# Weight rings begun one stage ahead, and a compression over 128 partitions, in a three-layer transformer kernel

## The reference

```python
mq, mk, mv, nq, nkv, ng = split(h @ w_in)            # layer 0: sparse mixer, 2840 columns
o = concat(moba_attention(...), nsa_attention(...)); o @ w_out
q, k, v = split(h @ w_in)                            # layer 1: difference attention, 3072 columns
# layer 2: gated delta rule over 512 positions; then 16,384 experts, 16 per head and token, by product keys
(silu(h @ w_gate) * (h @ w_up)) @ w_down             # feed-forward of layers 0 and 1, 2816 hidden

def nsa_compress(t, pos_emb, w1, w2):                # t: [b, g, S, 64]
    idx = arange(ncmp)[:, None] * 16 + arange(32)    # 15 blocks of 32 positions
    blocks = t[:, :, idx] + pos_emb
    hid = silu(einsum('bgnld,lde->bgne', blocks, w1))      # sum over 32 positions x 64 channels, e = 256
    return einsum('bgne,ed->bgnd', hid, w2)
```

## Time and profile before

| what | before |
|---|---|
| median of 3 runs | 2494.89 us |
| the profiled execution: its time, its span | 2503.65 us, 2501.9 us |
| PE (matmul) busy | 2059.2 us, 82% |
| PEld (weight load) busy | 1847.1 us, 74% |
| DVE busy | 1667.4 us, 67% |
| ACT busy | 934.1 us, 37% |
| POOL busy | 101.0 us, 4% |
| HBM read, mean rate | 363.87 MB, 150 GB/s |
| span of `cmp` | 183.3 to 276.3 us |

### The profile page before, as it was taken

How to read it: one execution, slowest core, us unless ns; L and a number is a source line. 1 busy time by engine, 2 the same in 40 slices (tenths; PEclk the granted TensorE clock), 3 DMA queues, 4 the chain that set the end, 5 groups by cost and what they waited for, 6 DMA issues and landing times. The chain is left out here.

```text
span 2501.9 us, 41554 instructions
## 1 busy us (share of the span) xinstructions
PE 2059.2 (82%) x16664; PEld 1847.1 (74%) x16664; DVE 1667.4 (67%) x2773; ACT 934.1 (37%) x1334; POOL 101.0 (4%) x92
## 2 busy tenths in 40 slices
PE   5838578996745999697887876899876999999997
PEld 2838358995735899486877765899865777999996
DVE  2562767876876786676356564389997777666665
ACT  1310434433342433333244452445465333444443
POOL 1000000000000000241000110000000000000000
PEclk9865699998967999898699887999999999999999
DMA  5707149875303884232000013377501666555554
GB/s 185 286 14 171 59 138 343 307 257 184 120 4 119 322 321 173 94 109 85 3 2 4 3 48 140 122 230 221 170 0 65 211 217 214 205 191 186 185 185 143
DMA packets 167334, 377.46 MB, mean 151 GB/s; under 512 B 12521, under 2 KB 111593, under 8 KB 154985
## 3 DMA queue, kind: packets, MB, share of 16 engines
q1 hardware_dynamic: 157794, 365.48, 42.6%
q10 hardware_dynamic: 9360, 9.44, 1.1%
HBM read 363.87 MB, written 11.01 MB: 150 GB/s over the span
## 5 line engine op out<-in xcount | busy, mean ns | idle before, releaser
L1136 DVE TENSOR_TENSOR experts_v_lo<-experts_v,experts_v_hi 128x1024 fp32r<-128x1024 f32 x128 | 156.8, 1225 | 98.9 <-ACT experts_v_hi L1110 98.5
L1084 PE MATMUL experts_py<-experts_v_hi,experts_c_hi 128*128 128x512 f32 x512 | 204.0, 398 | 20.9 <-DVE experts_v_lo L1136 20.7
L1110 ACT CAST experts_v_hi<-experts_v 128x1024 fp32r<-128x1024 f32 x128 | 134.3, 1049 | 220.9 <-PE experts_py L1088 112.6
L1291 PE MATMUL ffn_pa<-all_h_hi,ffn_u_hi 128*128 128x256 f32 x704 | 198.8, 282 | 21.4 <-DVE ffn_u_lo L1350 21.4
L1085 PE MATMUL experts_py<-experts_v_lo,experts_c_hi 128*128 128x512 f32 x512 | 201.4, 393 | 0.0
L1292 PE MATMUL ffn_pa<-all_h_lo,ffn_u_hi 128*128 128x256 f32 x704 | 198.3, 282 | 0.0
L1293 PE MATMUL ffn_pa<-all_h_hi,ffn_u_lo 128*128 128x256 f32 x704 | 198.2, 282 | 0.0
L1088 PE MATMUL experts_py<-experts_v_hi,experts_c_lo 128*128 128x512 f32 x512 | 158.5, 391 | 0.0
L2678 PE MATMUL route_pa<-all_h_hi,route_u_hi 128*128 128x256 f32 x512 | 146.8, 287 | 10.1 <-DVE route_u_lo L2563 10.1
L1291 PEld LDWEIGHTS ffn_pa<-all_h_hi,ffn_u_hi 128*128 128x128 f32 x704 | 134.5, 191 | 23.4 <-DVE ffn_u_lo L1350 21.9
L2679 PE MATMUL route_pa<-all_h_lo,route_u_hi 128*128 128x256 f32 x512 | 146.1, 285 | 0.0
(11 more groups left out here) (564 smaller groups left out, 5805.2 us busy)
## 6 DMA issues: line engine op xcount, KB each, us to landing
experts_v<-in_peer_v SPq DMA_DIRECT2D x128, 512.0 KB, 3.3
ffn_u<-in_ffn_columns SPq DMA_DIRECT2D x44, 1024.0 KB, 8.0
ffn_ada_w<-in_ada_w SPq DMA_DIRECT2D x36, 1024.0 KB, 5.7
route_u<-in_peer_u SPq DMA_DIRECT2D x64, 512.0 KB, 3.5
experts_u<-in_peer_u SPq DMA_DIRECT2D x64, 512.0 KB, 4.3
ffn_v<-in_ffn_rows SPq DMA_DIRECT2D x44, 512.0 KB, 8.5
proj_ada_w<-in_ada_w SPq DMA_DIRECT2D x12, 1024.0 KB, 6.3
proj_w<-in_diff_w_in SPq DMA_DIRECT2D x12, 1024.0 KB, 7.4
```

The source lines that it names most:

```text
L1084: pe.matmul(py[:, 2 * t + n, :], c_hi[:, b, part], v_hi[:, b, cols], start=start, stop=False)
L1136: dve.tensor_tensor(v_lo[:, i % 2, :], v[:, i % 2, :], v_hi[:, i % 2, :].bitcast(F32), ALU.subtract).then_inc(v_split, 1)
L1291: pe.matmul(out, u_hi[:, b, cols], h_hi[:, c, :], start=(c == 0), stop=False)
```

## The change

1. `Feed`: a ring (slots, their semaphores) that lives outside the stage that uses it. `feed.begin(sp)` issues the loads of all its slots from the stage ahead: `norm0`, `norm1`, `fnorm0`, `fnorm1`, `dcnorm`, `pnorm`, `attn` (for `out0`), `onorm1` (for `out1`), `dnv` (for `dngp`), `dnon` (for `dnout`). `out0` and `out1` have rings of 2 slots, in rows that are free at that time; the others keep 3.
2. The first chunk of `project`, `swiglu` and `peer_scores` is split in four pieces, each with its own steps on ScalarE and VectorE, and the first product waits for them one by one. With `h_t`, the casts of the activations go between the pieces. `high_w(0)` now stands ahead of `sums.move`. In `delta_qkv` the first cast goes ahead of the activations', and TensorE waits for these one by one.
3. `compress`: positions in pairs over 128 partitions (even ones on the lower 64, odd ones on the upper), so 2 x 2 x 16 matmuls of 128 rows; `blk` in 8 additions in place of 60; 16 turning matmuls (now plain ones, one for each half of the partitions) in place of 8 transposes; `cmp_w1` loaded whole (four loads of 1 MB) in `rope0`.
4. Modulation halves 14 to 17 move from `cmp` (10 to 6) to `proj0` (6 to 10).
5. `keep` is gone; its two stores stand behind the loads of `pq`.

```diff
+class Feed:
+    def __init__(self, st, name, sources, slots):
+        self.sources, self.slots, self.ring = sources, slots, len(slots)
+        self.loaded = [st.sem(f"{name}_loaded{i}") for i in range(self.ring)]
...
+    def begin(self, sp):
+        for j in range(min(self.ring, len(self.sources))):
+            self.load(sp, j)
 def project(nc, k, name, h_t, chunks, feed, residual=None, out=None, ada=None, row=None, loads=()):
+        def parts(j):
+            n = KT * chunks[j][2]
+            step = n // PIECES if j == 0 else n
+            return [slice(at, at + step) for at in range(0, n, step)]
         @block.sync
         def _(sp):
-            for j, (source, col, width) in enumerate(chunks):
+            for j in range(len(chunks)):
                 if j >= ring:
-                    sp.wait_ge(w_split, j - ring + 1)
-                sp.dma_start(w[:, j % ring, 0:KT * width], source).then_inc(slot_loaded[j % ring], 16)
+                    sp.wait_ge(w_split, PIECES + j - ring)
+                    feed.load(sp, j)
                 for n in halves_at(j, len(chunks)):
                     beside.load(sp, halves[n])
 def compress(nc, k, ins, z, q_t, pc_t, vc, gates, w1, w1_loaded, ada):
             for kv in range(2):
+                pe.wait_ge(blk_ready, 4 * (kv + 1))
+                pe.wait_ge(w1_loaded[kv], 32)
                 for e in range(2):
-                    for l in range(CMP_LEN):
-                        last = pe.matmul(ph[:, kv, e * N:(e + 1) * N], w1[:, l, e * P:(e + 1) * P],
-                                         blk[:, kv, l, :], start=(l == 0), stop=(l == CMP_LEN - 1))
+                    for l in range(L):
+                        last = pe.matmul(ph[:, kv, e * N:(e + 1) * N], w1[:, kv, l, e * P:(e + 1) * P],
+                                         blk[:, kv, l, :], start=(l == 0), stop=(l == L - 1))
-            fold(0, 6)
+            fold(0, 4)
...
-            fold(6, 7)
+            fold(4, 5)
...
-            fold(7, len(halves))
+            fold(5, len(halves))
 def sparse_layer(nc, k, ins, mod, next_mod, gains):
+                    normed(nc, k, "norm0", x, gains[:, 0:D], m[0], m[1], feeds=(feed,))
-                        out=z, ada=((ins["ada_w0"], ins["ada_b0"]), [(c, mod, 6 * D)], 8, 14))
+                            ada=((ins["ada_w0"], ins["ada_b0"]), [(c, mod, 6 * D)], 8, 18))
-                         ada=((ins["ada_w0"], ins["ada_b0"]), [(c, mod, 6 * D)], 14, 24))
+                         ada=((ins["ada_w0"], ins["ada_b0"]), [(c, mod, 6 * D)], 18, 24))
```

More of the change, by code:

```diff
@@ L309, in move, with slot, load, wait @@
             act.copy(self.row[:, j * CW:(j + 1) * CW], self.psum[:, n % self.banks, :]).then_inc(self.moved, 1)
+class Feed:
+    def __init__(self, st, name, sources, slots):
+        self.sources, self.slots, self.ring = sources, slots, len(slots)
+        self.loaded = [st.sem(f"{name}_loaded{i}") for i in range(self.ring)]
+    def slot(self, j):
+        return self.slots[j % self.ring]
+    def load(self, sp, j):
+        to = self.slot(j)[:, 0:self.sources[j].shape[-1]]
+        sp.dma_start(to, self.sources[j]).then_inc(self.loaded[j % self.ring], 16)
+    def begin(self, sp):
+        for j in range(min(self.ring, len(self.sources))):
+            self.load(sp, j)
+    def wait(self, engine, j):
+        engine.wait_ge(self.loaded[j % self.ring], 16 * (j // self.ring + 1))
+def ring_slots(st, name, columns, ring=3):
+    w = st.sb(name, [P, ring, columns])
+    return [w[:, i, :] for i in range(ring)]
+PIECES = 4
 def first_modulation(nc, k, name, weights, silu_c, row):
@@ L506, in _, with project @@
                 act.copy(*source(n)).then_inc(moved, 1)
-def project(nc, k, name, h_t, chunks, residual=None, out=None, ada=None, row=None, loads=()):
+def project(nc, k, name, h_t, chunks, feed, residual=None, out=None, ada=None, row=None, loads=()):
     with Stage(nc, name) as st:
@@ L524, in project @@
         psum = st.ps("psum", [P, 4, CW])
-        slot_loaded = [st.sem(f"slot_loaded{i}") for i in range(ring)]
         h_hi_ready, h_split, w_hi_ready, w_split, product, taken, scaled, moved = (st.sem(n) for n in (
@@ L735, in _ @@
         def _(sp):
-            sp.dma_start(pos_t[:], ins["cmp_pos"]).then_inc(loaded, 16)
+            for rows in sides:
+                sp.dma_start(pos_t[rows], ins["cmp_pos"]).then_inc(loaded, 16)
             sp.dma_start(w2[:], ins["cmp_w2"]).then_inc(loaded, 16)
-            for kv in range(2):
-                for e in range(2):
-                    cols = slice(e * P, (e + 1) * P)
-                    if kv:
-                        sp.wait_ge(e_sum, e + 1)
-                    sp.dma_start(w1[:, :, cols], ins["cmp_w1"][kv][:, :, cols]).then_inc(w1_loaded[e], 16)
-                beside.load(sp, halves[kv])
-            beside.load_bias(sp)
-            for half in halves[2:]:
+            for half in halves:
                 beside.load(sp, half)
-        @block.gpsimd
-        def _(pool):
-            beside.zero(pool)
         @block.tensor
@@ L887, in sparse_attention, with _ @@
         ends = [u for u, pair in enumerate(pairs) if pair[5] != "first"]
+        @block.sync
+        def _(sp):
+            for feed in feeds:
+                feed.begin(sp)
         @block.tensor
@@ L1653, in _ @@
         def _(pe):
-            pe.wait_ge(h_split, KT)
             for b in range(blocks):
@@ L2398, in delta_layer @@
                 h_t = sb.sb("h_t", [P, KT, XC])
+                feed = Feed(sb, "qkv", [ins["dn_w_qkv"][b] for b in range(3 * KT)],
+                            [free[:, i * D:(i + 1) * D] for i in range(1, 4)])
                 with Stage(nc, "dnc") as sc:
@@ L2488, in high_w @@
             def high_w(j):
-                act.wait_ge(slot_loaded[j % ring], 16 * (j // ring + 1))
+                feed.wait(act, j)
                 if j >= 2:
                     act.wait_ge(product, per * (j - 1))
-                act.copy(w_hi[:, j % 2, :], w[:, j % ring, :]).then_inc(w_hi_ready, 1)
+                for cols in parts(j):
+                    act.copy(w_hi[:, j % 2, cols], feed.slot(j)[:, cols]).then_inc(w_hi_ready, 1)
             high_w(0)
@@ L2781, in _ @@
                                          ALU.mult).then_inc(ready, 1)
-def keep(nc, copies):
-    with Stage(nc, "keep") as st:
-        stored = st.sem("stored")
-        block = st.block()
-        @block.sync
-        def _(sp):
-            for dram, tile in copies:
-                sp.dma_start(dram, tile).then_inc(stored, 16)
-            sp.wait_ge(stored, 16 * len(copies))
 def program(nc, ins, out):
```

281 lines of the change are left out of this document (163 added, 118 removed).

## The result

The changed kernel takes 2399.65 us (median of 4 runs, 2395.12 to 2400.89) against 2495.46 us for the kernel before in the same comparison (4 runs, 2494.06 to 2499.27). The ratio is 0.961, with a 95% interval of 0.9594 to 0.9627: 95.8 us less. The forecast was 2394 us, in a range of 2378 to 2412. The profiled execution, 2395.12 us, is the fastest of the four.

The account below looks back on a forecast made before the run. TensorE bounds product stages, with idle starts; half-clock sums, then small steps and folds, bound the compression. Savings 31.0 + 14.4 + 13.4 + 4.3 + 5.7 + 40.1 - 7.8 = 101.1 us take 2494.9 to 2394 us; range 2378 to 2412.

Parts of the forecast that it names:

- The heads: Starts of product stages: first product 1.6 us in, not 9.4; 7.8 us gained in each of four, 7.2 in out1 and dngp.
- pq: Start of pq, with keep in it: 14.97 us before the first product become 1.6, gain 13.4 us.
- The compression: cmp: 53 us in place of 93; start gains 4.8, sums take 27.4 for 54.8, tail gains 7.9; together 40.1 us.
- the row that I took against the rule: Compression's sums: profile row with 27.00 of 27.00 us busy at clock 0.50, so half clock was assumed for the new sums.
- SP's order in proj0: proj0: weight chunks behind modulation halves make TensorE wait at chunks 4, 6 and 10, 7.8 us in all; net gain 0.
- dnqkv: Start of dnqkv: weight cast first, first product 3.9 us in instead of 8.2, gain 4.3 us.
- out0 and dnout: Starts of out0 and dnout: row sums stay ahead, first product at 7.2 us in out0; gains 2.7 and 3.0 us.
- A: Rival, chance 0.12: no waits in proj0 because transfer pairs land 3 us sooner, so its head is a gain too; 2386 us.
- C: Rival, chance 0.06: cmp_w1 or the new matmuls hold the compression's sums at 54.8 us, 27.4 lost; 2421 us.
- D: Rival, chance 0.05: early transfers land late or stage ends wait for them; about 45 us saved, 2450 us.
- E: Rival, chance 0.02: slower than before, half clock for most of a long stage, 154 us over 22 ffn0 tiles; 2548 us.
- B: Rival, chance 0.08: TensorE keeps full clock across shorter gaps, saving 2.3 us at each of nine starts, 21 us; 2373 us.

Follow-up runs that it names:

- late_loads: Changed kernel with each of the ten rings begun in its own stage instead of the stage ahead: 2448.18 us (0.9804 of before).
- whole_first: Changed kernel where, in five stages, VectorE waits for all four pieces of the first cast and TensorE for all four differences: 2416.02 us (0.968 of before).
- keep_back: Changed kernel with the two stores in a stage of their own ahead of pq again: 2406.32 us (0.9649 of before).
- wide_cols: Changed kernel where the compression's 64 sum matmuls move their 30 columns four times over (120 columns): 2385.3 us (0.9569 of before).
- halves_back: Changed kernel with modulation halves 14 to 17 back in cmp (proj0 adds 6, cmp 10): 2398.2 us (0.9607 of before).
- best: Changed kernel with weight loads ahead of modulation halves, swap, dnqkv's first two differences on VectorE, out0/dnout row-sum copies between ScalarE's pieces: 2361.51 us (0.9469 of before).
- best_wide: As best, with wide_cols in place of swap and dngate's 32 columns also moved four times over: 2352.1 us (0.9429 of before).
- swap: Changed kernel with the compression sums' operands exchanged, blocks (30 columns) loaded and w1 (256 columns) moving: 2389.98 us (0.9585 of before).

## Why the prediction was right

**The heads** held, term by term. 1.6 us was forecast, 1.69 measured; 2.2 and 2.37 in `out1` and `dngp`. The plain heads gave 6.8, 8.8 and 8.3 us instead of 7.8 each, and the difference is the clock's beginning, which I had put at 1 us either way: TensorE's work at half clock goes from 4.2 to 6.0 us in `ffn0`, from 5.9 to 3.4 in `proj1` and from 5.8 to 4.4 in `ffn1`, and each of these microseconds costs half of one. late_loads and whole_first show both parts of the reason.

**pq** gave 12.8 us for 13.4, and keep_back puts 5.5 of them to the stage `keep`.

**The compression**, 39.4 us for 40.1, was right as a sum with three parts that were each off a little. The sums took 27.5 us for 27.4. The start gave 3.1 us instead of 4.8: they begin 7.9 us into the stage, as VectorE waits for the small transfers, of which there is one more. The tail gave 9.0 instead of 7.9. On the clock, the row that I took against the rule was right for this kernel: 27.5 us of work without a pause at 0.50. The Trainium skill's rule that activity releases the clock ("TensorE: Matmul & The Clock Gate", Part 1) did not hold here for a TensorE that was merely never idle; once the same matmuls moved 120 columns, in wide_cols, it did. The 13.7 us that the prediction worked out by that rule and set aside could be had after all: in wide_cols `cmp` is 13.9 us shorter.

**SP's order in proj0** was read rightly out of the trace of before: waits at chunks 4, 6 and 10, 2.2, 3.4 and 2.2 us forecast, 3.40, 1.43 and 2.11 measured, 6.9 for 7.8, and none with six halves, as halves_back shows. The three places and the sum were right, the sizes one by one were not. The step that failed is "So `proj0` starts 7.8 us earlier and ends where it did": it ends 3.1 us later. I had given the waits no price in clock. The first is followed by 3.4 us at 0.50, the last jobs run at 0.50 from 141.7 us on, and the head is 1.6 us longer at 0.50 than before, so TensorE's work at half clock grows from 6.0 to 13.3 us. With its waits the stage loses 10.7 us.

**dnqkv** is the term that was mis-sized, 1.9 us for 4.3. I had taken 2.4 us for GpSimd's difference and 0.6 for each of VectorE's as if they ran beside each other. The first product came at 4.46 us instead of 3.9, and TensorE waited 1.54 us more in its first block.

**out0 and dnout** gave 2.5 and 3.9 for 2.7 and 3.0. Their first products came at 6.5 and 7.2 us for 7.2. That both fit so well is in part luck: in the seven other traces in which the heads have the same code the products come at 6.9 to 7.9 and at 6.5 us, and against the one trace of before `out0` gains 0.5 to 2.7 us and `dnout` 5.6. `out0` would have gained 3 us more, but its fourth chunk stands behind a half just as in `proj0`, which I had not looked for with a ring of two slots.

Of the rivals, A, C and D are excluded by the waits, by the 0.215 us of a record and by the table; E came in none of the four executions. B fell for this kernel: each of its product stages still has 2.8 us or more at half clock. `ffn0`'s half-clock work went from 4.2 to 6.0 us in this trace and is 3.4 to 5.2 in the others. TensorE is idle for about 3 us in front of most first products. Where it is idle for less, the rival's mechanism can be seen: over the wait of 2.81 us in `out0` the clock stays at 1.00 in this trace and falls to 0.50 in the seven others with the same code, and with the 0.73 us of best it doesn't fall in either of two traces (best and best_wide). Over the whole kernel TensorE's work at half clock went down from 255 to 199 us, 27 of these 56 in the sums (211 to 232 in the seven other versions that keep the sums as they are, so this trace had luck). What sets where in a stage the clock rises stays open; it moved between executions of the same code by 2 to 3 us.

The saving was 101.1 us by the forecast and 96.5 by the table. The errors that matter are 3.1 us for `proj0` and 2.4 for `dnqkv`, both too favourable. The others are 1.0 us at most and nearly cancel; they are of the size by which the clock moves a stage by chance.

## What to carry to other kernels

Where one queue issues what the bound engine needs and what may wait, put the first ahead in the list at every step: a load that waits for a consumer holds up all behind it, and a free slot of the ring doesn't help (in `proj0` it had been free for 11 us). When work is moved to another place, look at which engines it now meets there (VectorE and GpSimd above all), and count an earlier first product as a gain only for the idle time that it removes. And look at the granted clock of stretches where TensorE is busy with narrow matmuls: at 0.50 it can pay to move columns that nobody needs, as it did here by 14.4 us and again in `dngate` by 8.

## What was not expected of the hardware

- Matmuls with 128 loaded columns and 30 moving kept a TensorE that was busy all the time at the half clock for 27.5 us; the same with 120 moving had it for 4.4 us and then ran at 0.112 us a record, from one start to the next. Moving 32 columns four times over in `dngate` did the same.
- A plain float32 matmul with 256 moving columns costs 0.43 us a record at half clock and 0.22 at the full one (swap), and has two records; a matmul of the split products (fp32r) has one, of 0.213 and 0.119 us from one start to the next in `proj0` before. The 0.116 of the earlier trace rows is 10.00 / 86 and counts the records at both edges of the stretch.
- A subtraction of VectorE that meets one of GpSimd that is under way takes 2.43 to 2.84 us instead of 0.68.
